# The last token tile's rows of u by picks instead of dense products, in a hybrid decoder block

## The reference

```python
q = (xt @ w_q).reshape(T, PEER_HEADS, 2, PEER_QDIM // 2)          # 8 heads
s = jnp.einsum('thpd,hpkd->thpk', q, sub_keys)                    # 2 x 128 keys
s_top, i_top = lax.top_k(s, PEER_TOPK)                            # 16 of 128, twice
cand_s = s_top[:, :, 0, :, None] + s_top[:, :, 1, None, :]
best_s, best_pos = lax.top_k(cand_s.reshape(T, PEER_HEADS, 256), PEER_TOPK)
idx = jnp.take_along_axis(cand_i, best_pos, axis=-1)              # of 16384 experts
g = jax.nn.softmax(best_s, axis=-1)
h = jnp.einsum('td,ted->te', xc, jnp.take(u, ic, axis=0))         # 128 picks a token
a = jax.nn.gelu(h, approximate=False) * gc
y = jnp.einsum('te,ted->td', a, jnp.take(v, ic, axis=0))
```

## Time and profile before

| what | us (or as said) |
|---|---|
| median of the runs (3) | 3083.79 (3082.13 to 3088.96) |
| the profiled execution | 3081.31 |
| its span, first to last instruction | 3079.6 |
| TensorE, VectorE, ScalarE, GpSimd busy | 2968.7, 2313.1, 977.5, 1257.6 |
| moved by DMA | 601.37 MB, 195 GB/s over the span |

### The profile page before, as it was taken

The page is one execution under the profiler, slowest core; times in us unless marked ns, Lnnn a source line. Parts: engine busy times, 40 slices in busy tenths (PEclk is TensorE's granted clock), DMA queues, the critical chain, the costliest instruction groups (busy, mean ns, idle before and its releaser), DMA issues. The chain is left out here.

```text
span 3079.6 us, 46779 instructions
## 1 busy us (share of the span) xinstructions
PE 2968.7 (96%) x17450; PEld 1663.7 (54%) x17450; DVE 2313.1 (75%) x4663; ACT 977.5 (32%) x1417; POOL 1257.6 (41%) x883
## 2 busy tenths in 40 slices
PE   7989998989999799999999999999999999999999
PEld 4445465455555577777765555555555544444444
DVE  3255376358888666666649999989999999999996
ACT  4332365134433344444432222222222222222221
POOL 1013121014243311211226666676666666566562
PEclk9999899999999899999999999999999999999999
DMA  3110100121211245545568989989999888888884
GB/s 101 55 55 15 55 1 28 62 74 63 83 56 61 93 166 198 189 176 199 188 227 290 310 302 329 316 303 315 307 308 322 290 312 296 303 298 299 300 299 168
DMA packets 258490, 601.37 MB, mean 195 GB/s; under 512 B 21025, under 2 KB 127665, under 8 KB 255281
## 3 DMA queue, kind: packets, MB, share of 16 engines
q1 hardware_dynamic: 181168, 321.78, 31.0%
q0 software_dynamic: 73728, 268.47, 24.3%
q10 hardware_dynamic: 3456, 9.44, 0.8%
HBM read 516.78 MB, written 82.84 MB: 195 GB/s over the span
## 5 line engine op out<-in xcount | busy, mean ns | idle before, releaser
L238 PE MATMUL f_y<-f_v_hi,f_a_hi 128*128 128x512 f16 x1536 | 582.4, 379 | 8.7 <-DVE p_h L2323 8.7
L239 PE MATMUL f_y<-f_v_lo,f_a_hi 128*128 128x512 f16 x1536 | 582.1, 379 | 0.0
L240 PE MATMUL f_y<-f_v_hi,f_a_lo 128*128 128x512 f16 x1536 | 582.1, 379 | 0.0
L2292 POOL DMA_INDIRECT x_rows<-in_peer_v,p_row_index x256 | 305.9, 1195 | 281.6 <-DVE p_h L2342 256.2
L2292 POOL DMA_INDIRECT x_rows<-in_peer_u,p_row_index x251 | 321.7, 1282 | 186.4 <-DVE x_rows L2332 141.9
L2332 DVE SCALAR_TENSOR_TENSOR x_rows<-x_rows,p_xs 128x1024 f32<-128x1024 f32 x256 | 378.4, 1507 | 24.7 <-DMA x_rows<-in_peer_u,p_row_index 24.5
L2342 DVE SCALAR_TENSOR_TENSOR p_h<-x_rows,f_row_a,p_h 128x1024 f32<-128x1024 f32 x256 | 384.5, 1502 | 16.6 <-DMA x_rows<-in_peer_v,p_row_index 11.4
L2301 POOL TENSOR_TENSOR f_v_lo<-f_v_in,f_v_hi 128x1024 f16<-128x1024 f32 x128 | 286.8, 2241 | 87.4 <-ACT f_v_hi L2240 85.4
L2323 DVE SCALAR_TENSOR_TENSOR p_h<-f_y,p_h 128x512 f32<-128x512 f32 x384 | 262.4, 683 | 75.9 <-PE f_y L240 75.4
L238 PE MATMUL f_hid<-p_act_hi,x_u_hi 128*128 128x384 f16 x880 | 286.9, 326 | 2.1 <-DVEq L2308 2.1
L240 PE MATMUL f_hid<-p_act_hi,x_u_lo 128*128 128x384 f16 x880 | 286.9, 326 | 0.0
(11 more groups left out here) (314 smaller groups left out, 5489.5 us busy)
## 6 DMA issues: line engine op xcount, KB each, us to landing
f_v_in<-in_peer_v SPq DMA_DIRECT2D x128, 512.0 KB, 5.6
dense_weights<-e_stage SPq DMA_DIRECT2D x24, 2048.0 KB, 7.6
f_g_in<-dense_weights SPq DMA_DIRECT2D x32, 1536.0 KB, 16.2
x_u_in<-in_peer_u SPq DMA_DIRECT2D x56, 512.0 KB, 6.2
x_gel<-early_tiles SPq DMA_DIRECT2D x72, 384.0 KB, 3.5
e_u_in<-in_peer_u SPq DMA_DIRECT2D x48, 512.0 KB, 4.1
early_tiles<-e_gel SPq DMA_DIRECT2D x48, 384.0 KB, 2.3
a_w_in<-in_w_in SPq DMA_DIRECT2D x24, 512.0 KB, 3.7
```

What stands on the lines that cost most here:

```text
L238: pe.matmul(out, a_hi, b_hi, start=first, stop=False)
L239: pe.matmul(out, a_hi, b_lo, start=False, stop=False)
L240: return pe.matmul(out, a_lo, b_hi, start=False, stop=last)
L2292: nc.gpsimd.indirect_dma_start(out=rows[q % ROWS][:], out_offset=None, in_=table, in_offset=bass.IndirectOffsetOnAxis(ap=T.row_index[:, ti ...
```

## The change

The last token tile (tile 7, `HT`, "held") is no longer dense in its **hidden** values, only in its outputs. Its rows of u are gathered by picks, 128 jobs of one indirect DMA and one VectorE instruction. The dense hidden products cover five tiles (HID = 640 tokens, in halves of 320) instead of six.

- `project_out` keeps the normed rows of tile 7 in `T.xs_h`.
- `retrieve`: once a head's picks are known, VectorE makes the indices (`index_held`). 28 jobs (HELD_JOBS) run in heads 2 to 6, in pairs: after the first sorting (slot 0), after the second (slot 1) and at the end of the head (slot 2). GpSimd fetches them into two buffers: slot 0 ahead of the head's first `low`, slot 1 behind `weights`, slot 2 behind its last `low`. A fetch waits until the job that used the buffer before is done.
- `spread_weights`: the other 100 jobs run between the first 146 of 192 steps, on the five buffers that the experts use afterwards. The low half of the early tiles moves from GpSimd to VectorE, straight from PSUM (`low_from_bank`), and ScalarE's full copy goes; the two `left` products become one instruction of 1024 elements. After the last job ScalarE applies Gelu to the 128 sums, VectorE multiplies by the weights, TensorE transposes, ScalarE copies the result into the place of the tile's weights, so that the last two blocks of the table hold finished values a instead of weights.
- `experts`: Gelu, its product with the table, and the kept tiles are 640 wide; ScalarE copies the 128 columns of the held tile from the table (`held`), ahead of `hi_a`. Output products stay 768 wide.

The diff's core:

```diff
@@ retrieve
+            def fetch(h, slot):
+                for q in jobs(h, slot):
+                    pool.wait_ge(held_index, q // TOPK + 1)
+                    if q >= 2:
+                        pool.wait_ge(held_sum, q - 1)
+                    nc.gpsimd.indirect_dma_start(
+                        out=rows[q % 2][:], out_offset=None, in_=io.peer_u[0],
+                        in_offset=bass.IndirectOffsetOnAxis(ap=T.h_index[:, q:q + 1], axis=0)).then_inc(
+                            held_loaded[q % 2], 16)
             for h in range(PEER_H):
                 of_head = tiles(h)
+                fetch(h, 0)
                 E.low(pool, *of_head[0])
...
                     E.low(pool, c, b)
-                    if h and i == 0:
-                        weights(h - 1)
+                    if i == 0:
+                        if h:
+                            weights(h - 1)
+                        fetch(h, 1)
+                fetch(h, 2)
...
+            def held_jobs(h, slot):
+                for q in jobs(h, slot):
+                    dve.wait_ge(held_loaded[q % 2], 16 * (q // 2 + 1))
+                    nc.vector.scalar_tensor_tensor(rows[q % 2][:], rows[q % 2][:], 1.0, T.xs_h[:], ALU.mult, ALU.mult,
+                                                   accum_out=T.h_hid[:, q:q + 1]).then_inc(held_sum, 1)
@@ spread_weights
+        HBLOCK = HAT // BLOCK - 1
+        UJOBS = PICKS - HELD_JOBS
+        JOB_STEPS = HBLOCK * STEPS + 2
...
-                nc.vector.tensor_tensor(left[r][:, 0], same[s % 2][:], each(w_hi), ALU.mult)
-                nc.vector.tensor_tensor(left[r][:, 1], same[s % 2][:], each(w_lo), ALU.mult).then_inc(built, 1)
-                for q in range(SPREAD_JOBS * n // ALL, SPREAD_JOBS * (n + 1) // ALL):
-                    row_job(q)
+                nc.vector.tensor_tensor(left[r][:], lanes(same[s % 2][:], 1, P, 2, P, BANK_T),
+                                        lanes(w[:, :, toks], 2, P, 2, P, BANK_T), ALU.mult).then_inc(built, 1)
+
+                if n % 4 == 0 and n // 4 < EARLY_S * NBLOCK:
+                    E.low_from_bank(dve, *ring_at(n // 4 // EARLY_S, n // 4 % EARLY_S))
+                if n < JOB_STEPS:
+                    for q in range(UJOBS * n // JOB_STEPS, UJOBS * (n + 1) // JOB_STEPS):
+                        row_job(q)
+                if n == HBLOCK * STEPS + 8:
+                    weigh_held()
+                if n == (HBLOCK + 1) * STEPS - 1:
+                    split_held()
...
+            def turn_held(blk):
+                pe.wait_ge(h_a_done, 1)
+                pe.wait_ge(E.u_lo_done, BASE + (blk + 1) * EARLY_S)
+                pe.transpose(E.u_ps[:, 0, :], T.h_hid[:], T.ident[:]).then_inc(h_turned, 1)
+                pe.wait_ge(h_out, 1)
...
+            def gelu_held():
+                act.wait_ge(row_used, UJOBS)
+                nc.scalar.activation(T.h_hid[:], T.h_hid[:], ACT.Gelu).then_inc(h_gelu, 1)
+
+            def held_out():
+                act.wait_ge(h_turned, 1)
+                nc.scalar.activation(w_t[:, HAT:], E.u_ps[:, 0, :], ACT.Copy, scale=S_A).then_inc(h_out, 1)
@@ experts
-                    toks = slice(NS * P + half * DHALF, NS * P + (half + 1) * DHALF)
+                    toks = slice(NS * P + half * HHALF, NS * P + (half + 1) * HHALF)
...
+            def held(n):
+
+                m = n % LOOP
+                g, j = m // GROUP, m % GROUP
+                act.wait_ge(g_loaded[g], n // LOOP * 16 + 16)
+                act.wait_ge(a_lo_done, BASE + n - 1)
+                nc.scalar.activation(gel[m % 2][:, HID:].rearrange("p (b t) -> p b t", t=TB),
+                                     g_in[g][:].rearrange("p b (i t) -> p b i t", t=TB)[:, HID // TB:, j, :],
+                                     ACT.Copy).then_inc(held_done, 1)
```

More of the change, by code:

```diff
@@ L1929, in _ @@
             E.turn(pe, 0, 0)
[L1930 removed]
+            with pe.Fori(0, HBLOCK) as blk:
                 step(blk, False)
[L1932 removed]
+            step(HBLOCK, False, held=True)
+            for blk in range(HBLOCK + 1, NBLOCK):
+                step(blk, blk == NBLOCK - 1)
             def turn(b):
```

162 lines of the change are left out of this document (113 added, 49 removed).

## The result

The changed kernel takes 3063.96 us (median of five, 3051.26 to 3069.79), the kernel before 3085.91 (five, 3082.13 to 3088.96). The ratio is 0.9927, 95% interval 0.9909 to 0.9945: about 22 us faster, where I had forecast 74 and a range that ended at 3055. The sign was right, the size was not, and the time lies 9 us above the range. Times of one and the same kernel scatter: the changed kernel's over 18.5 us, those of the kernel before, with all its runs beside the experiments, over 20.

What follows compares the result with a forecast made beforehand. TensorE bounds the spread and late turns; the search loops through four engines. Search +2, spread -20, late turns -52, early turns -3, join -1: -74 us from 3081.3 gives 3007, plus 2.5 for the median: 3010 us, range 2980 to 3055.

Steps and rivals of the forecast that it cites:

- The spread: Spread stage: VectorE becomes the bound of the first 146 steps, TensorE's shorter products set the rest; -20 us.
- rival D: Spread: the merged `left` falls to one element per cycle, 3092 us, slower; chance 0.06.
- E: Spread: GpSimd holds VectorE's row jobs, +2.0 us for each of 100, 3210 us, slower; chance 0.03.
- The search: Search for picks: TensorE's gain nearly offset by VectorE's added jobs and waits; +2 us, bounds -2 and +12.
- the gain on TensorE is 20 us in all: Search: only the first half's 0.64 us counts per tile, 1.28 for a head's last tile; 20 us in all.
- the lag of 8 us after head 6: Search: delay from added jobs and gather waits, 8 us after head 6, of which 2 us remain after the last head.
- Rival C: Search: second and third pairs of every head wait for their rows, six us per iteration, 3040 us; chance 0.07.
- The late turns: Experts' late turns: TensorE 15.16 us a tile, VectorE 14.75 plus 0.67 of row waits, so 15.4; -52 us.
- the two signs that I had named for being wrong: Search growing by over 12 us, or TensorE in the late turns waiting for VectorE over 1 us per tile.
- The early turns: Experts' turns without hidden products: VectorE's `gel` product loses 0.13 us a tile; -3 us, bounds 0 and -9.
- A: Late turns: TensorE keeps the pace, 16 us more gained, 2994 us; chance 0.12.
- B: Late turns: VectorE or the gathers bind at the old pace, +52 us, 3062 us; chance 0.11.

Runs made afterwards that it cites:

- s6_second_first: Changed kernel with only the gathers of each head's second pair moved directly behind the picks on GpSimd: search 368.9 us, against 398.5.
- l1_no_product: Changed kernel with the experts' products of all gathered rows of tiles 0 and 1 cut to one column: late turns 810.7 us, against 858.3.
- l3_thirds: Changed kernel with only its 1.5 MB table loads cut into thirds: 3038.27 us, ratio to before 0.9841, late turns 848.3 us.
- e4_small_table: Changed kernel with late table loads after the first loop cut to one block of 24: late turns 824.2 us, against 858.3.
- c2: Changed kernel with both pairs' gathers moved on GpSimd, 20 row jobs moved to the spread's end, table loads in thirds: 2988.49 us, ratio to before 0.9678.
- c3: Changed kernel with only the second pair's gathers moved, 20 row jobs moved to the spread's end, table loads in thirds: 2988.78 us, ratio to before 0.9691.
- both moves: Changed kernel with first-pair gathers behind the first tile's `low` and second-pair gathers directly behind the picks: search 373.5 us, against 398.5.
- s3_neither: Changed kernel without 26 of the search's 28 gathers and with its 28 products cut to one column: search 373.4 us, against 398.5.

## Why the prediction failed where it did

**The spread: right.** -17.6, with the join -19.1, against -20. VectorE did become the bound: between 1081 and 1450 it is busy for 367.08 of 369 us. The job steps ended about 388 us after the start of the stage, forecast 385. The merged `left`, forecast at 0.69:

```profile
L1985 DVE TENSOR_TENSOR e_left<-e_same,e_w x192: 675/679/686, 1082.3 to 1569.4; 128x1024 f16<-128x1024 f16 x192
```

So rival D (one element per cycle) is out, and so is E: none of the 100 jobs took over 1.22 us beside GpSimd's gathers. This was the best-founded term, one engine's instructions added up with nothing else in their way.

**The search: two steps failed.** The first is "the gain on TensorE is 20 us in all". I had seen that TensorE waits for `low`, and counted only the first halves for it, but not asked what that chain hangs on behind GpSimd. In head 3 it goes back to VectorE's `top_f`, which no column shortens; measured with neither gathers nor products were 3.4 us. The second is the lag of 8 us after head 6 and its absorption to 2. For head 2 the sum was good: I had put the end of its iteration at about 802, and it stood at 801.84. But I let the later heads win some of it back, "from head 3 on the rows arrive before the 30 us of sorting are over". They didn't: VectorE's second pair waited 12.3 us in head 2 and 1.7 to 2.9 in each of heads 3 to 6 too, 21.5 in all, and the five heads together grew by 24, after head 1 had been 3.9 shorter. So the lag after head 6 was 20 us and not 8. Rival C had named this wait, at 6 us per iteration and 0.07; it came near in the sum, while half of it stood in head 2. VectorE's own iteration (48.5 by my sum) is what `s6_second_first` shows, 47.8 to 48.9. What failed was holding it to be what the loop would run at, with the gathers where the change puts them. The last head absorbed nothing either: from head 6's `find` to `same` 78.6 us against 77.4. In the short form of the search it absorbed 6.6 (70.8 us), as I had forecast, of a lag of 17; there the size of the lag alone is what failed.

**The late turns: one step failed.** Both paces were right, TensorE's 15.16 (`l1_no_product`) and VectorE's 14.75 (tiles of 14.7 in the trace). The failed step is "its waits for gathered rows, 0.67 us, are on the path: 15.4", and 15.45 with the higher DMA share. Two things were wrong in it. The waits grew to 0.95 us a tile, which by the same sum gives 15.7. And the sum adds means: measured are 16.09, 0.4 more. I spread the waits evenly over the tiles; most come in one tile of four, about 4 us at once. Between two of them VectorE gets back 15.16 - 14.75 = 0.4 us a tile, 1.2 in three, so that some 3 us per group reach TensorE; four tiles take 4 x 16.09 = 64.4 us where TensorE needs 60.6. Before it got back 16.44 - 14.88 = 1.56 a tile, 4.7 in three, and that covered it. The already showed the form: 24.5 us in 13 waits, the longest 3.8, in 48 tiles with 12 table loads. I read the total and not the count. But the form is not all of it: with even waits (`l3_thirds`) the mean is still 15.97, 0.3 above the same sum, and without the table's bytes (`e4_small_table`) it is 15.45 where both engines' own sums stay below 15.2. That TensorE and VectorE then take turns, which I had named only for the lower bound, would fit this; no run parts it out.

Of the two signs that I had named for being wrong, the first appeared (the search grew by over 12 us, in this trace), the second did not: TensorE waited 32.7 us for VectorE over some 49 tiles, 0.7 a tile and not over 1.

**The early turns.** -0.2 and not -3. In neither kernel do VectorE's 0.13 us per tile show; 6 us were to be had there from the table loads, in both kernels.

**The rivals.** A (TensorE keeps the pace) needed slack on VectorE and a smooth load, and came near only in c2 and c3, with a VectorE that had 20 jobs less. B (the late turns keep the old pace) went too far: 18.6 us were kept, 1.4 under my lower bound of 20 for that term. Its time, 3062, is within 2 us of the measured one, but by luck, since it had the search at +2 and no gain in the late turns. Its cause, the DMAs, was in part right: they don't set the pace, but the table loads make the rows late. The range ended at 3055 because I took B out almost whole; the time was 3064.

## What to carry to other kernels

When a change takes slack from the engine that follows the bounding one, list that engine's waits by length and period: a rare long wait that the slack repaid over several tiles is paid for the most part afterwards. Cutting the transfer behind it into pieces helps in so far as there is slack for the shorter waits: here it brought 10 us alone and 20.6 once VectorE had 20 jobs less. An added transfer belongs in the queue at the first place at which its buffer is free and nothing more urgent stands behind it, not behind the operation that happens to precede its user; with the second pair's gathers moved, ten in all, the search was 25 to 30 us shorter (14 to 18 against its short form). And a load issued too early is no better: it holds up its queue for the wait on its buffer.

## What the runs showed of the hardware

- Beside a tensor operation of GpSimd, VectorE's operations with two SBUF inputs stretch by microseconds: a job of 1.23 us to 5.09, an operation of 0.29 to 3.80. In the rows above they end 0.15 us (the small ones) or 1.1 us (the job) after GpSimd's operation, as if they ran only once it was over. One with a single input does the same: the cast of `top_f` (L1767, kernel before) takes 0.29 us alone and 2.86 to 3.26 beside GpSimd's operations in four heads, and ends 0.15 us after them. Gather issues of GpSimd don't do that: the 100 jobs of the spread took 1.205 to 1.217 us. I knew the first from one row and had counted it only for the spread.
- A 1.5 MB table load delays the gathers beside it: 9.6 us from issue to landing in place of 5.9 (medians, kernel before).
- The changed kernel's search, unedited, had three lengths: 398.5, 398.3 and 398.4 us in three runs, 387.3 in two, 392.4 in one. How much of the 18.5 us by which the changed kernel's times differ this makes is not known: only one of these executions has a trace, and the kernel before scatters as much with a search of 376.8 and 376.7 in its two traces (one with its table loads in thirds). In the runs of 387 the first `find` of head 6 comes at 999 and not at 1002.6, before GpSimd's `low` at 1002.7, and doesn't collide with it; a difference of 3.6 us there becomes 11 by the end. What decides between them is open. With both moves the search took 373.5, 373.4 and 373.7, with the second alone 368.9 and 368.8.
- After a wait TensorE runs at its lower level for a while: in `s3_neither` a 320-column matmul takes 0.45 us after the wait of 7.53 us shown above, at a granted clock of 0.50 (820 to 822), and 0.31 after one of 1.04; from 826 on the granted clock is 1.00 again. In the search the granted clock fell from 1.00 to 0.94 with the change, so that its waits cost more than their own time; how much more was not measured.
